# Second feed-forward, input projection: 512 token columns in one matmul, or in two of 256

## What is computed

```
D_FF = -(-8 * D_MODEL // (3 * 256)) * 256        # 2816

def swiglu_ffn(h, w_in, w_out):
    gate, up = jnp.split(h @ w_in, 2, axis=-1)
    return (jax.nn.silu(gate) * up) @ w_out
...
        h = rmsnorm(x, norm_g[i, 2]) * (1.0 + scale) + shift
        y = swiglu_ffn(h, f_w_in[i], f_w_out[i])
        x = x + gate * rmsnorm(y, norm_g[i, 3])
```

## Time and profile before

| | us |
|---|---|
| median of 3 runs | 2212.21 (2212.01 to 2213.32) |
| span of the profiled execution | 2209.9 |
| PE busy | 2167.0 (98%), 10456 matmuls |
| DVE busy | 1203.4 (54%) |
| ACT busy | 999.4 (45%) |
| POOL busy | 973.0 (44%) |
| the changed loop, 1085.7 to 1303.3 us | 217.6 |

### The profile page before, as it was taken

The page is one execution under the profiler, slowest core; times in us unless marked ns, Lnnn a source line. Parts: engine busy times, 40 slices in busy tenths (PEclk is TensorE's granted clock), DMA queues, the critical chain, the costliest instruction groups (busy, mean ns, idle before and its releaser), DMA issues.

```text
span 2209.9 us, 29015 instructions
## 1 busy us (share of the span) xinstructions
PE 2167.0 (98%) x10456; PEld 1756.4 (79%) x10456; DVE 1203.4 (54%) x1720; ACT 999.4 (45%) x1425; POOL 973.0 (44%) x421
## 2 busy tenths in 40 slices
PE   7999999999999999999999999999999899999998
PEld 5788888888878777778888888888777688888886
DVE  5877665521176877886522221240888755666522
ACT  4324544334445655654543434453555644444332
POOL 3544444446644333334544456666122143444563
PEclk8999999999999999999999999999999999999999
DMA  7653475553315344333232323344221132333232
GB/s 316 221 209 124 147 272 218 178 161 97 115 58 194 115 148 157 115 124 96 77 95 95 96 74 101 109 122 155 87 70 42 36 105 86 104 95 95 79 97 72
DMA packets 74338, 273.88 MB, mean 124 GB/s; under 512 B 8632, under 2 KB 11320, under 8 KB 67849
## 3 DMA queue, kind: packets, MB, share of 16 engines
q1 hardware_dynamic: 70872, 266.77, 36.5%
q10 hardware_dynamic: 3376, 5.90, 0.8%
HBM read 269.24 MB, written 8.12 MB: 126 GB/s over the span
## 4 chain that ended last, share of the span: by engine, by line
PE 76%; issue 14%; POOL 5%; DVE 3%; ACT 1%; DMA 1%; ACTq 0%; SPq 0%; POOLq 0%; DVEq 0%
PE bank L557 61%; POOL wlo L518 5%; PE bank L974 4%; PE bank L1066 2%; PE bank L580 2%; PE bank L1031 1%; PE bank L995 1%; PE bank L622 1%; PE bank L1014 1%; PE bank L584 1%; PE bank L630 1%; PE bank L669 1%; DMA ada_first<-ada_d 1%; DVE x L1624 1%; PE bank L915 1%
## 5 line engine op out<-in xcount | busy, mean ns | idle before, releaser
L518 POOL TENSOR_TENSOR wlo<-raw,whi 128x1024 fp32r<-128x1024 f32 x382 | 927.6, 2435 | 1146.7 <-ACT whi L1104 1146.4
L1104 ACT ACTIVATE whi<-raw 128x1024 fp32r<-128x1024 f32 x382 | 400.5, 1055 | 560.3 <-PE bank L557 537.8
L557 PE MATMUL bank<-h_hi,whi 128*128 128x512 f32 x1608 | 633.0, 394 | 1.9 <-POOL wlo L518 1.9
L557 PE MATMUL bank<-h_hi,wlo 128*128 128x512 f32 x1608 | 626.5, 390 | 0.0
L557 PE MATMUL bank<-h_lo,whi 128*128 128x512 f32 x1608 | 625.8, 389 | 0.0
L557 PEld LDWEIGHTS bank<-h_hi,whi 128*128 128x128 f32 x1608 | 301.9, 188 | 68.3 <-issue 6.3
L557 PEld LDWEIGHTS bank<-h_hi,wlo 128*128 128x128 f32 x1608 | 301.8, 188 | 64.0
L557 PEld LDWEIGHTS bank<-h_lo,whi 128*128 128x128 f32 x1608 | 302.0, 188 | 61.6
L557 PE MATMUL bank<-g_hi,whi 128*128 128x512 f32 x592 | 230.4, 389 | 0.0
L557 PE MATMUL bank<-g_hi,wlo 128*128 128x512 f32 x592 | 230.3, 389 | 0.0
L557 PE MATMUL bank<-g_lo,whi 128*128 128x512 f32 x592 | 230.3, 389 | 0.0
(11 more groups left out here) (357 smaller groups left out, 2985.2 us busy)
## 6 DMA issues: line engine op xcount, KB each, us to landing
raw<-f_in_d SPq DMA_DIRECT2D x88, 512.0 KB, 3.5
raw<-m_d SPq DMA_DIRECT2D x65, 512.0 KB, 3.6
ada_f<-ada_d SPq DMA_DIRECT2D x24, 1024.0 KB, 7.0
raw<-g_in_d SPq DMA_DIRECT2D x44, 512.0 KB, 3.5
raw<-w_in_d SPq DMA_DIRECT2D x41, 512.0 KB, 3.6
csb<-cs_d SPq DMA_DIRECT2D x32, 640.0 KB, 6.3
ada_a<-ada_d SPq DMA_DIRECT2D x16, 1024.0 KB, 4.9
raw<-a_in_d SPq DMA_DIRECT2D x24, 512.0 KB, 6.0
```

The source lines that it names most:

```text
L518: nc.gpsimd.tensor_tensor(wlo[:, s], raw[:, s], whi[:, s].bitcast(F32), ALU.subtract).then_inc(lo_ready, 1)
L557: mm = nc.tensor.matmul(psum[bank][:], w[:, s, kk, :], xs[part == "lo"][:, k, :], start=first and kk == 0 and i == 0, stop=last and kk == ...
L1104: nc.scalar.activation(whi[:, s], raw[:, s], ACT.Copy).then_inc(hi_ready, 1)
```

## The change

The loop of ffn(1) calls a new function halved in place of single. It has the same waits ahead of the tile and the same signal with its last matmul. Each product of a k tile is written as two matmuls with the same weights, the first for the token columns 0 to 255, the second for 256 to 511, into the two halves of the same bank. The first matmul of a tile alone has start set, stop stands at both halves of the last product. The four interleaved tiles ahead of the loop, the first feed-forward, the third and all other projections stay as they are.

```diff
+            def halved(name, u, it, n):
+
+                b = bank_of(T0[name] + u, it, n)
+                c = C0[name] + u
+                pe.wait_ge(lo_ready, c + 1 + it * n)
+                for k in range(CH):
+                    for i, (w, part) in enumerate(PRODUCTS):
+                        for half in range(2):
+                            cols = slice(S // 2 * half, S // 2 * (half + 1))
+                            mm = nc.tensor.matmul(psum[b][:, cols], w[:, c % RING, k, :], (h_hi, h_lo)[part == "lo"][:, k, cols],
+                                                  start=k == 0 and i == 0 and half == 0, stop=k == CH - 1 and i == 2,
+                                                  skip_group_check=True)
+                mm.then_inc(chunk_done, 1)
+
...
                     four("f_in1", 3)
                     with pe.Fori(0, 10) as it:
                         for u in range(4, 8):
-                            single("f_in1", u, it, 4, wait=False)
+                            halved("f_in1", u, it, 4)
```

## The result

The changed kernel takes 2225.69 us (median of 4 runs, 2223.88 to 2227.78) against 2212.11 us (4 runs, 2211.16 to 2213.32): a ratio of 1.0061, 95% interval 1.0047 to 1.0075, 13.6 us more. Forecast were 2218.6 us and a range from 2213.0 to 2225.5. The profiled execution of the changed kernel is the longest of its four runs, 2227.78 us.

A forecast was written before the change was run, and what follows sets the result against it. PE alone was taken to bound the loop. Extra weight loads, sequencer and other engines were costed at nothing; 960 pairs at +6.7 ns gave +6.4 us on 2212.2 us, so 2218.6 us, range 2213.0 to 2225.5 us.

The forecast's parts named there:

- What bounds the stage: In the loop at lines 734 to 736 only PE sets the end; pitch 226.7 ns over 960 matmuls, 217.60 us.
- The weight load: In the loop, 960 more loads, each hidden beside the streaming; about 111 ns is the floor of the pitch.
- The loss beside the columns: In the loop a half takes 116.7 ns, as at line 915; a pair costs +6.7 ns, x 960 = +6.4 us.
- the bounds: For the loop's loss term: above, halves at 120.0 ns, +12.8 us; below, 113.3 ns, nothing, or the 111 ns floor, -4.5 us.
- The test with the full load under line 915's last product: A full tile's load under the last product of a line 915 group takes no longer: 1536.04 to 1536.16.
- The upper bound: In the loop each matmul on a full weight tile loses a fixed 13.3 ns: a half 120.0 ns, +12.8 us.
- Rival 1: The full fixed loss on each of the loop's matmuls: +12.8 us, 2225.0 us; chance 0.18.
- Rival 2: In the loop the loss goes with the columns, a half 113.3 to 115.5 ns: 0 to 4.4 us, say 2214; chance 0.22.
- Rivals 3 to 5: Halves at 111 ns floor, 2207.7 us (0.03); sequencer too slow, 2234.6 us (0.05 with serial load); second halves' loads left out.
- The range: Kernel time 2213.0 to 2225.5 us, reaching over most of rival 2 and all of rival 1.
- the sign of being wrong in kind: PE idle before line 583's loads, or a stage other than the loop moving by over 1 us.
- the sum: Whole kernel: span 2209.9 us plus 6.4 gives 2216.3; with 2.3 us around the span, 2218.6 us, 0.29% slower.

The follow-up runs named there:

- the groups: Changed kernel with halves only for k tiles 0, 1, 4 and 5, whole matmuls for the others, all 128 weight columns: loop 225.7 us, time 2222.93 us.
- exchanged roles: Changed kernel with 256 columns of the weight ring as moving data and 64 columns of h as weights: loop 217.7 us, time 2211.09 us.
- the mixture of widths: Changed kernel with first halves on all 128 weight columns and second halves on the first 64: loop 224.1 us, time 2214.08 us.

## Why the prediction was right or wrong

**What bounds the stage: right.** PE was busy for the whole loop in every variant. In the runs that were repeated the loop's 12.8 us came out at the end of the kernel (+13.6 and +13.0 us); in the single runs the time follows the loop only as closely as the clock lets it.

**The weight load: right.** It is made again for the second half, beside the stream, and its floor of 111 ns was measured at 111.7. The Trainium skill, "TensorE: Matmul & The Clock Gate", section "The mechanism", has the sentence that a load overlaps a matmul in flight only where the row groups differ, and ahead of it in the same section that a load into the background weight buffer is pulled ahead too. The trace after is against the first: a product costs 13.3 ns more, not 111.

**The loss beside the columns: wrong, and it is the error.** The step was "I take 116.7 ns for a half, the nearest row", from line 915. In the loop a half takes 120.0 ns, so the term was 13.3 ns x 960 = +12.8 us and not +6.4; the other 0.7 us between 2218.6 and 2225.69 are within the scatter. The row was near in the number of columns but not in two other things: its weights start at odd places, which moves 113.4 ns to 117.1 (62 and 64 weight columns), and they are narrower, which at odd places makes 1.7 ns (117.1 against 118.8) and at regular ones 6.6 (113.4 against 120.0). The two differences pull in opposite directions, and it is chance that they left the row between the bounds. The test with the full load under line 915's last product, which I took as evidence that width does not matter, showed one single step of 0.12 us in a place with steps of 113 to 122 ns; one step read to a hundredth of a microsecond can't tell 117 from 120. The average of the row itself was read rightly: 116.4 and 116.7 ns from two groups, 117.0 over all eight.

**The upper bound was the answer.** Rival 1, a fixed 13.3 ns for each matmul on full weights, gave 2225.0 us for 0.18; the loop's 230.4 us was its figure, 230.5 was measured. Its argument, that every 512-column matmul on such weights shows 13.3 ns, came from the very tiles and engine of the loop. As an explanation it does not hold: a price of each matmul on full weights would give 240.0 ns for the cut at 248 too, which takes 236.3, and 226.7 for the whole matmuls between the groups, which take 231. It came out for equal halves at regular places; that it did there is in part luck.

**Rival 2, the loss going with the columns: wrong.** It needed 113.3 ns with full weights; that pitch showed only with 62 and 64 weight columns. The rule of the Trainium skill, "TensorE: Matmul & The Clock Gate", section "Back-to-back issue gap", 2.5 ns beside the columns, was weighed with it; the section calls it the gap of an isolated matmul. No run here shows 2.5 ns: the least loss on average was 6.7 ns, with halves on 62 and 64 weight columns.

**Rivals 3 to 5: wrong.** The floor was not reached on average with 256 columns, the sequencer kept up even at 111.7 ns over 3840 matmuls, and the loads were not left out.

**The range.** Its end at 2225.5 us was rival 1's 2225.0 us with half a microsecond on it. It left out that the granted clock moves a run, so a true cost of 12.8 us is read as anything from 2223.88 to 2228.03 us in the ten runs of the changed kernel. A range that takes a rival in has to take in its scatter too. The same holds for the sign of being wrong in kind, another stage moving by over 1 us: the stretches before and behind moved by 1.5 and 1.7 us in the first pair of profiles, and the clocks above show that this was scatter and no new mechanism. A small slip beside it: what lies around the span is 1.8 to 1.95 us in every execution that has both numbers; the 2.3 us of the sum set a median against the span of one execution.

**What stays open.** What the loss is. It is steady and large (13.3 ns) or steady and small (6.7 ns) for some combinations of length and width at regular places, and goes in repeated patterns of unequal steps for others, mostly between the two but 16.7 ns for whole matmuls with 64 weight columns. The order of halves does not touch it, nor do exchanged roles with 64 weight columns; the starts of the weight tiles and the cut of the columns do. That could be the reads of weights and of moving data getting into each other's way by address and time, but this is a guess: no run shows such a conflict, the patterns of 5 and of 42 steps follow no address alone, and the mixture of widths (116 to 117 ns behind either) fits neither the load's own width nor the next one's. So it is shown that the term was mis-sized and which row misled it, and not why a matmul on these tiles loses 13.3 ns.

## What to carry to other kernels

Where PE is the bound and runs without a pause, cutting matmuls on full 128x128 weights into halves cost 13.3 ns a product here, against 213.3 ns for its columns, and cutting them into quarters cost 220, since each piece brings a full load, one every 112 ns. So keep the columns of a matmul at their maximum with such weights. To price a matmul that the trace does not show, look for rows with the same weight width, the same length and the same layout of the tiles, and where no row has all three, take the nearest of each as the ends and not one as the middle. Neither row alone is safe: the loss of the same tiles at another length was right here with 128 weight columns, and would be wrong with 64 (16.7 ns at 512 columns, 6.7 at 256). A pitch wants many steps: one row of the timeline, rounded to 0.01 us, does not carry a difference of 3 ns.

## What was not expected of the hardware

- Fewer weight columns do not make a matmul cheaper in order: with 256 columns streamed a half takes 117.8, 113.4, 116.0 and 120.0 ns for 32, 64, 96 and 128 weight columns; with 512 streamed 64 columns take 230.0 ns and 128 take 226.7. So with 64 weight columns two halves are 3.2 ns cheaper than one whole matmul.
- Weight tiles at odd starts (248 bytes apart) make halves slower with 62 columns (117.1 against 113.4 ns) and, with the roles exchanged as well, faster with 128 (118.8 against 120.0).
- Cutting 512 columns at 248 instead of 256 takes 236.3 ns instead of 240.0.
- Whole matmuls between groups of halves take 231 ns each where a row of them alone takes 226.7.
- Where the steps are unequal they repeat in fixed patterns, of 5, 6, 42 or 48 steps, and not all of these fit the places of the operands.
